# Block 2 head outputs copied whole and moved by DMA, and the softmax reciprocal made on GpSimd as a power of minus one

## What is computed

```python
# A and B (block 1), per head and block of 128 queries
p = softmax(scores (+ sink or bias))
y = p @ v
# L (block 2), per layer
sc = einsum('bhqd,bhkd->bhqk', q_blk, k) * scale
p  = softmax(sc)
o  = einsum('bhqk,bhkd->bhqd', p, v)            # head outputs
y_a = (o * silu(z_a)) @ w_attn_proj
```

## Time and profile before

| | us |
|---|---|
| median of 3 runs (1490.05 to 1491.66) | 1491.34 |
| the profiled execution's own time | 1491.93 |
| its span | 1490.1 |
| PE busy | 1463.4 (98%) |
| DVE busy | 816.5 (55%) |
| ACT busy | 623.6 (42%) |
| POOL busy | 336.4 (23%) |
| granted TensorE clock, mean | 0.997 of full |

### The profile page before, as it was taken

One profiled execution on the slowest core, in us unless ns is written; L12 is line 12 of the kernel. 1 busy time (PEld: TensorE's weight loads), 2 busy tenths in 40 slices (PEclk: granted clock), 3 DMA queues, 4 the chain that ended last, 5 costly groups with the idle time before them and its releaser, 6 DMA issues.

```text
span 1490.1 us, 18694 instructions
## 1 busy us (share of the span) xinstructions
PE 1463.4 (98%) x7077; PEld 1219.3 (82%) x7077; DVE 816.5 (55%) x1326; ACT 623.6 (42%) x963; POOL 336.4 (23%) x322
## 2 busy tenths in 40 slices
PE   9999999999999999999999999999999999999998
PEld 7887888888888888888888787888888878788886
DVE  5648844344443434334578795434447879544344
ACT  5427843234322313234444785323333468533232
POOL 2004510112000000002308854100110846320012
PEclk9999999999999999999999999999999999999999
DMA  5554332323323232232232003232323200232321
GB/s 199 75 129 120 101 96 85 112 86 108 101 85 110 88 111 86 93 104 85 68 109 85 1 1 113 85 113 86 108 69 113 85 1 2 86 113 85 113 85 58
DMA packets 157359, 132.48 MB, mean 89 GB/s; under 512 B 34840, under 2 KB 151840, under 8 KB 157280
## 3 DMA queue, kind: packets, MB, share of 16 engines
q1 hardware_dynamic: 157120, 131.35, 29.4%
q10 hardware_dynamic: 160, 0.07, 0.0%
HBM read 125.30 MB, written 2.92 MB: 86 GB/s over the span
## 4 chain that ended last, share of the span: by engine, by line
PE 87%; DVE 8%; POOL 2%; ACT 1%; issue 1%; DMA 0%; DVEq 0%; ACTq 0%; SPq 0%; POOLq 0%
PE G L1800 74%; PE G L1782 4%; DVE sq L1408 2%; PE S L1782 2%; POOL t L799 2%; PE T L1891 1%; PE G L1978 1%; PE G L1911 1%; PE G L1918 1%; DVE ab L1287 1%; DVE pt_l L1434 1%; DVE z L1422 1%; DVE pt L1434 0%; DMA raw<-in_w_in 0%; PE G L1984 0%
## 5 line engine op out<-in xcount | busy, mean ns | idle before, releaser
L1800 PE MATMUL G<-gx,w 128*128 128x512 f32 x3024 | 693.8, 390 | 0.4 <-DVE w L1270 0.4
L1800 PEld LDWEIGHTS G<-gx,w 128*128 128x128 f32 x3024 | 566.7, 188 | 119.5 <-issue 1.4
L1270 DVE TENSOR_TENSOR w<-raw,w 128x2048 fp32r<-128x2048 f32 (+1 forms) x110 | 252.9, 2299 | 223.4 <-ACT w L960 223.4
L960 ACT ACTIVATE w<-raw 128x2048 fp32r<-128x2048 f32 x112 | 211.6, 1890 | 135.7 <-PE G L1800 109.4
L1800 PE MATMUL G<-kvb,w 128*128 128x512 f32 x960 | 218.4, 389 | 0.0
L1800 PEld LDWEIGHTS G<-kvb,w 128*128 128x128 f32 x960 | 180.2, 188 | 37.4
L799 POOL TENSOR_TENSOR t<-t,rden 128x512 f32<-128x512 f32 (+2 forms) x128 | 108.9, 854 | 153.0 <-DVE rden L1414 151.0
L835 POOL TENSOR_TENSOR t<-sig 128x512 f32<-128x512 f32 x24 | 35.4, 1473 | 357.4 <-DVE sig L1482 357.4
L1545 DVE TENSOR_TENSOR x<-G,x 128x512 f32<-128x512 f32 x56 | 38.6, 689 | 115.3 <-PE G L1800 115.3
L1022 ACT ACTIVATE t<-sq,nm 128x512 f32<-128x512 f32 (+3 forms) x128 | 80.1, 626 | 22.3 <-DVE nm L1408 21.3
L1800 PE MATMUL G<-m,w 128*128 128x512 f32 x384 | 87.4, 389 | 0.0
(11 more groups left out here) (227 smaller groups left out, 1769.4 us busy)
## 6 DMA issues: line engine op xcount, KB each, us to landing
raw<-in_w_in SPq DMA_DIRECT2D x98, 512.0 KB, 7.2
raw<-in_w_up SPq DMA_DIRECT2D x32, 512.0 KB
raw<-in_w_down SPq DMA_DIRECT2D x32, 512.0 KB
raw<-in_w_out SPq DMA_DIRECT2D x24, 512.0 KB
raw<-in_w_attn_proj SPq DMA_DIRECT2D x8, 512.0 KB
raw<-in_w_fourier_proj SPq DMA_DIRECT2D x8, 512.0 KB
biasb<-bias_rows SPq DMA_DIRECT2D x24, 128.0 KB
xin<-in_x SPq DMA_DIRECT2D x4, 512.0 KB, 6.4
```

The source lines that it names most:

```text
L960: nc.scalar.activation(K.w[:, j % 2, 0, 0:n], K.raw[:, j % 2, 0:n], ACT.Copy).then_inc(K.w_hi, 1)
L1270: nc.vector.tensor_tensor(K.w[:, s, 1, 0:n], K.raw[:, s, 0:n], K.w[:, s, 0, 0:n].bitcast(F32), ALU.subtract).then_inc(K.w_lo, 1)
L1800: mm = nc.tensor.matmul(b[:, :], w(p, k), x(q, k), start=(k == i == 0), stop=(k == kts - 1 and i == len(PASSES) - 1))
```

## The change

- In all attentions DVE's reciprocal is gone. POOL waits for `exp_ok` itself, raises `den` to the power of `minus_one` (a constant column) with a `tensor_tensor` of 128x1, waits for that result, and scales as before.
- In L, ACT copies the whole bank (128 partitions) into `halves`. SP moves the two halves with two DMAs into `z` and `z_low`. POOL adds `z_low` to `z` once for two heads: behind blocks 14, 22 and 30, and for the last pair after the attention. DVE has no part in it any more. `half_out` now counts `tile_out`.
- `halves` and `z_low` lie in the idle slot `raw[1]`, those of the last pair in the arena. Slab j+12 therefore waits for the third sum.
- ACT's last `half_out` of a layer stands in front of the load of the sigmoid table instead of behind it.

```diff
@@ program_sync
         slab(j0 + 10, columns(w_in, ZA0))
+        def z_halves(h):
+            t, e, A = h // 2, h % 2, Heads(K, "L", l)
+            r = slice(e * HD, (e + 1) * HD)
+            sp.wait_ge(K.tile_out, (A.g_out(h) + 1).value())
+            if e == 0 and t == 2:
+                sp.wait_ge(K.z_sum, l * HALF + t - 1)
+            halves, z_low = out_halves(K, t)
+            for to, half in ((K.z[r, t, :], halves[0:HD, e, :]), (z_low[r, :], halves[HD:P, e, :])):
+                sp.dma_start(to, half).then_inc(K.z_in[e], 16)
+
+        for h in range(HEADS - 1):
+            z_halves(h)
         slab(j0 + 11, columns(w_in, ZA0 + SCOL), Num(U_L // 2 + UL // 2, (l, UL // 2)))
+        z_halves(HEADS - 1)
+        sp.wait_ge(K.z_sum, (l + 1) * HALF - 1)
@@ program_pool
+            pool.wait_ge(K.exp_ok, (A.u0 + n + 1).value())
+            d = slice(n % 4, n % 4 + 1)
+            nc.gpsimd.tensor_tensor(K.rden[:, d], K.den[:, d], K.minus_one[:, :], ALU.pow).then_inc(K.rden_ok, 1)
             pool.wait_ge(K.rden_ok, (A.u0 + n + 1).value())
             p = K.t[:, n % 3, c]
...
+            if A.kind == "L" and n in SUM_AT:
+                z_summed(A.layer, SUM_AT.index(n))
...
+    def z_summed(l, t):
+        for e in range(2):
+            pool.wait_ge(K.z_in[e], 2 * 16 * (l * HALF + t + 1))
+        nc.gpsimd.tensor_tensor(K.z[:, t, :], K.z[:, t, :], out_halves(K, t)[1], ALU.add).then_inc(K.z_sum, 1)
...
         for t in range(HALF):
+            if t == 2:
+                z_summed(l, HALF - 1)
@@ program_act
         def half_out(h):
             act.wait_ge(K.pv_done, A.pairs(2 * h + 1).value())
-            nc.scalar.activation(K.z[h % 2 * HD:(h % 2 + 1) * HD, h // 2, :], K.G[A.g_out(h) % GB][0:HD, :],
-                                 ACT.Copy).then_inc(K.z_half, 1)
+            moved = 2 * 16 * (A.layer * HALF + h // 2)
+            if moved:
+                act.wait_ge(K.z_in[h % 2], moved)
+            nc.scalar.activation(out_halves(K, h // 2)[0][:, h % 2, :], K.G[A.g_out(h) % GB][:, :], ACT.Copy).then_inc(K.tile_out, 1)
...
+        if A.kind == "L":
+            half_out(A.total // TT - 1)
         load_table(ACT.Sigmoid)
-        (half_out if A.kind == "L" else out_hi)(A.total // TT - 1)
+        if A.kind != "L":
+            out_hi(A.total // TT - 1)
@@ program_vector
-        def rden(n):
-            c = slice(n % 4, n % 4 + 1)
-            dve.wait_ge(K.exp_ok, (U + n + 1).value())
-            nc.vector.reciprocal(K.rden[:, c], K.den[:, c]).then_inc(K.rden_ok, 1)
...
-            if A.kind == "L":
-                dve.wait_ge(K.z_half, (A.layer * HEADS + h + 1))
-                nc.vector.tensor_tensor(K.z[r, t, :], psum(g)[HD:P, :], K.z[r, t, :], ALU.add).then_inc(K.tile_out, 1)
-                return
...
-            if A.last_of(n) is not None:
+            if A.kind != "L" and A.last_of(n) is not None:
                 out(A.last_of(n))
-            if n + 2 < total:
-                rden(n + 2)
             low(n)
```

More of the change, by code:

```diff
@@ L99 @@
 HEAD_ROOT = 4
+SUM_AT = (14, 22, 30)
 GAIN_AT = {2: (0, 1, 2, 3), 3: (4, 5, 6, 7)}
@@ L226, in allocate @@
     K.zeros = sb("zeros", [P, 1], F32)
-    K.spare = sb("spare", [P, 1], F32)
+    K.minus_one = sb("minus_one", [P, 1], F32)
     K.unused = sb("unused", [P, 1], F32)
@@ L277, in allocate @@
     K.m2 = at("m2", 24, [P, 2, KT, SEQ], F32R)
+    K.halves = at("halves", 0, [P, 2, SEQ], F32, raw0 + SLAB * 4)
+    K.z_low = at("z_low", 4, [P, 2, SEQ], F32, raw0 + SLAB * 4)
+    K.last_halves = at("last_halves", 24, [P, 2, SEQ], F32)
+    K.last_z_low = at("last_z_low", 28, [P, SEQ], F32)
     K.G = [ctx.enter_context(nc.psum_tensor(f"G{i}", [P, 512], F32)) for i in range(GB)]
@@ L330, in allocate @@
     K.exp_ok = semaphore("exp_ok")
+    K.minus_ok = semaphore("minus_ok")
     K.rden_ok = semaphore("rden_ok")
@@ L361, in allocate @@
     K.y_hi = semaphore("y_hi")
-    K.z_half = semaphore("z_half")
+    K.z_in = [semaphore(f"z_in{i}") for i in range(2)]
+    K.z_sum = semaphore("z_sum")
     K.ab_hi = semaphore("ab_hi")
@@ L782, in program_pool @@
     nc.gpsimd.memset(K.ones[:, :], 1.0).then_inc(K.ones_ok, 1)
+    nc.gpsimd.memset(K.minus_one[:, :], -1.0).then_inc(K.minus_ok, 1)
     def sums(norm):
@@ L895, in program_pool @@
     nc.gpsimd.memset(K.pt["A"][0][:, :, 2, 0, :].bitcast(F32), 0.0).then_inc(K.pt_zero, 1)
+    pool.wait_ge(K.minus_ok, 1)
     probabilities(Heads(K, "AB"))
@@ L931, in program_pool @@
             pool.wait_ge(K.pool_ok, Num(4 + 2 * t + 1, (l, 12)).value())
+            if t in (0, HALF - 1):
+                pool.wait_ge(K.z_sum, l * HALF + (HALF - 1 if t == 0 else HALF))
             nc.gpsimd.tensor_tensor(K.t[:, t % 3, :], K.sq[:, t % 2, :], K.z[:, t, :],
@@ L1443, in attention @@
             scores(n)
-            if n:
-                rden(n - 1)
             if n == 0 and first is not None:
@@ L1456, in attention @@
                 scores(n + AHEAD)
-            if A.last_of(n) is not None:
+            if A.kind != "L" and A.last_of(n) is not None:
                 out(A.last_of(n))
-            if n + 2 < total:
-                rden(n + 2)
             low(n)
-        out(total // TT - 1)
+        if A.kind != "L":
+            out(total // TT - 1)
     def merge(sig, dst, j, g, f, h, mix, sig0, pair_, first=None):
@@ L2146, in ab_columns, with out_halves @@
     return slice(0, SCOL) if half else slice(0, P)
+def out_halves(K, t):
+    if t == HALF - 1:
+        return K.last_halves, K.last_z_low[:, :]
+    return K.halves, K.z_low[:, t % 2, :]
 def fourier_tile(grp):
```

## The result

The changed kernel takes **1501.26 us** (median of 4 runs, 1500.76 to 1501.67), the kernel before 1491.03 in the same comparison: ratio 1.0072, 95% interval 1.0059 to 1.0085. It is slower by 0.7%. The forecast was 1485.5; of the rivals, POOL as the bound is the one whose sign and cause came, though not where it had put them.

A forecast was written before the change was run, and what follows sets the result against it. PE was taken as the bound, waiting 0.49 us a head of L for POOL's late scaling. Gains of 3.8 us in L and 2.1 in A brought 1491.93 to 1486.0, less 0.6 for the median: 1485.5 us; 8-in-10 range 1480 to 1506.

The forecast's parts named there:

- POOL as the bound: Rival: long powers make POOL the bound in L and B from q = 0.50; 1506 us at q = 0.61; chance 0.30.
- q: Duration of one 128x1 power on POOL, 128 times in all; taken as 0.30 us, between 0.19 fixed and 0.61.
- 1483.5 us for q = 0.19: Whole kernel: the time estimated if a power cost only the fixed part, following the Trainium skill's dispatch rule.
- L, throughput: Heads of L: POOL needs 7.17 us, below PE's 7.46, so PE becomes the bound and 0.49 us is gained whole.
- 5.97 + 4q: POOL's time for a head of L; it meets PE's 7.46 us at q = 0.37 and today's 7.95 at 0.50.
- L, gain of the new outputs: Steady heads of L: transposes start 0.49 us earlier for each of six heads, 2.9 us gained in each layer.
- L, end: Last blocks of L: z sum and a power ahead of block 31's scaling cost 1.0 us in each layer.
- A: Attention A: scaling starts at 139.27 instead of 139.56, 0.3 us gained for each of about seven heads, 2.1 us.
- Nothing in sum: Attention B: the power comes behind the preceding scaling; one head's loss is offset by other heads' gains, so no change.
- ACT, the copies, DVE: L: ACT's copy takes 0.59 us, copies land in 3.2 us, DVE falls from 7.56 to 6.2 us a head.
- Each further 0.1 us costs some 12 us: Whole kernel, in the rival with POOL as the bound: the price of a longer power, with 1506 us at q = 0.61.

The follow-up runs named there:

- e4: The changed kernel with a product by minus one (ALU.mult) in place of each power on POOL, so no reciprocal is computed; 1482.8 us.
- e9: The changed kernel with a second, unused power over 4 or 32 columns added on POOL in one block of eight; one run, 1556.9 us.
- e2: The changed kernel with the reciprocal back on DVE, keeping the new head outputs; 1488.2 us.
- e5: The changed kernel with the reciprocal back on DVE and the third z sum behind block 31 instead of 30; 1485.1 us.
- e6: The changed kernel with the third z sum behind the scaling of block 31 instead of 30; 1495.2 us.
- e3: The changed kernel with POOL's power in L only and DVE's reciprocal in A and B; 1495.4 us.
- e7: The changed kernel with two products on 128x1 in place of each power on POOL, so no reciprocal is computed; 1486.5 us.
- e10: e5 with POOL making the reciprocal in B alone, for blocks 0 and 1 of every four; 1489.3 us.
- e11: e5 with POOL making the reciprocal in B alone, for blocks 2 and 3 of every four; 1485.6 us.

## Why the prediction was wrong, point by point

- **q, the step that failed.** "q = 0.30 us, nearer to the fixed part because there is only one element". It was 0.55, near the upper bound of 0.61. Of the missing 0.25 most is start: a power has 0.40 us ahead of its element, a product 0.19. The fixed part of another operation of the same engine was no measure for it. With q = 0.19 the three stretches gain 9.2 us in e4's profile instead of losing 8.2. (The 1483.5 us for q = 0.19 is not what the prediction's own terms give, which is about 1484.5; e4 also gained 0.1 us a head in B, which the terms had at nothing.) The Trainium skill's rule (GPSIMD Engine Reference, Performance versus the Vector engine), a fixed dispatch and some 12 cycles for an element even with branches, gave less still; e9's 158 ns for an element stands against it for this operation.
- **L, throughput.** The line 5.97 + 4q gives 8.16 us for a head at q = 0.55, over today's 7.95. Measured were 7.3 to 7.4 without a z sum and 8.5 with one. The line spreads four sums over eight heads, but only two stand inside L, and the third at its end; and from one scaling to what follows it only 1.00 us pass, not 1.04. By the rows POOL needs 4 x (0.62 + 1.00) + 0.79 = 7.3 us without a sum, just PE's pace. So POOL bound the heads with a sum and the last blocks, and not all of L.
- **L, gain of the new outputs.** 0.49 us a head was somewhat small: in e2, e4 and e5 a head takes 7.32 us, 0.64 less than before. Less the end, e4, with the whole scheme, gained 2.2 and 3.1 us in the two L, against 2.9 less 1.0. That PE's wait was POOL's lateness, and not its own weight loads, is shown by e5, whose PE runs without a gap there.
- **L, end.** Forecast: the last scaling 1.0 us later, by the sum and one power ahead of block 31. PE waited 2.20 us there instead of 0.28, and 0.97 in e6 without the sum: POOL needs 1.62 us for each of the last blocks and arrives late from them too. This took back the whole lead of 0.90 us and 1.07 more. In the first layer TensorE's granted clock then fell to 0.50, its lower level of 1.2 GHz, after PE had stood idle those 2.2 us, and the eight matmuls at 912.19 took 2.08 us instead of the 1.22 of the kernel before (window, kernel after):

```profile
912.00:914.30 2.30, 2.16 (x10) 2.11 (x10) 0.14 (x1) 0.00 (x0) 0.00 (x0) 0.50 0.00 0
```

  In the second layer PE stood idle 2.19 us at the same place, and the clock stayed at 1.00. In e3 it fell in the second layer alone (2.20 and 2.19 us idle), in e4 in the first alone (1.51 in both), in e7 in neither (1.90 in both). So the idle time alone doesn't decide it, and what does stays open.

- **A.** By the prediction's own line, 138.83 + 0.07 + 0.55 + 0.07 = 139.52 against 139.56: nothing gained. Measured: about 0.1 us a head lost.
- **B, a second failed step.** "Nothing in sum" counted one power ahead of one scaling. Its rival's line, 2.47 + 0.28 + 4 x 0.55 = 4.95 against 4.71, gives 0.24 a head; 0.55 was measured. The loop with two powers, which e10 and e11 isolate, is what both left out.
- **ACT, the copies, DVE.** ACT's copy of 128 partitions took 0.60 us, as taken. The copies landed after 2.3 us in the median, earlier than the 3.2 assumed; one of the last pair took 6.5, and still no z sum waited (0.0 idle in its group). DVE was to fall from 7.56 to 6.2 us a head of L and came to 6.6: the z sum took its 0.69 along, the four reciprocals only 0.07 each and not 0.16, since they had begun together with the accumulator's read ahead of them (both at 861.24 in the kernel before). That is still below PE's 7.3, so nothing hangs on it.
- **The rival.** "Each further 0.1 us costs some 12 us", 1506 at 0.61: its line gives 1498.4 at 0.547; the kernel took 1501.3. That it comes so near is luck. It would have 5.8 us lost in L (0.21 x 16 and twice 1.24 at the ends) and 1.8 in B; the profiles have 2.9 in L and 5.3 in A and B.

## What to carry to other kernels

Before moving a small operation to another engine, price that very operation on it, with a kernel of its own if no row shows it: here 0.36 us on a 128x1 tile was worth 18 us, 128 times over. Then count it twice, in the engine's sum for a step and in the closed loop of buffers that sets the step's pace; here sixteen powers in the loop cost 4.3 us on an engine with slack, and beside the loop 0.1. And look at the last blocks of a loop by themselves: there L lost what its heads had gained. Work that others do not await goes behind the last thing they do await, as the third z sum does in e5.

## What the runs showed of the hardware

A float power on POOL takes 0.40 us and 0.16 for each element of a partition (e9); the median of the 128 in the kernel after is 0.547.

The last z sum of each layer took 3.37 us where the six others took 1.27 (kernel after, DVE and POOL, first layer):

```profile
931.34 2.29 DVE L1317 TENSOR_TENSOR w<-raw,w 128x2048 fp32r<-128x2048 f32 x1 [5.22 <-ACT w L1002]
931.41 3.37 POOL L913 TENSOR_TENSOR z<-z,last_z_low 128x512 f32<-128x512 f32 x1
```

In both layers a DVE instruction of 2.29 us had begun just before; from its end to POOL's end are 1.15 and 1.16 us, so POOL seems to have stood still for most of it. One of the 128 powers took 1.00 us instead of 0.55, and beside it lies the same pattern, with a low part of DVE that took 0.98 us where it took 0.68 in the kernel before, with POOL idle (kernel after):

```profile
120.77 0.61 POOL L828 TENSOR_TENSOR t<-t,rden 128x256 f32<-128x256 f32 x1
120.95 0.98 DVE L1330 TENSOR_TENSOR kvb<-sumsq,kvb 128x512 fp32r<-128x512 f32 x1
121.34 1.00 POOL L825 TENSOR_TENSOR rden<-den,minus_one 128x1 f32<-128x1 f32 x1
```

The Trainium skill (SBUF — State Buffer, Who interferes with whom) says that a VectorE instruction with two SBUF inputs contends with a GpSimd one that reads SBUF, that the port pair they share is an exclusive lock, and that the order of issue decides who is blocked; these rows agree. No run separates the instructions on purpose, so the cause is only argued.
